# Turning the MLP operand row tile by row tile behind the out-projection, and computing two of three token bands of the first up product there

## The reference

```python
o = jnp.concatenate([group_rms(oa), group_rms(ob), group_rms(oc)], axis=-1) * g_out
x = layer_norm(ALPHA * x + g1 * (o @ w_out)) * ln1_g + ln1_b
u = layer_norm(x) * (1 + sc2) + sh2
f = jnp.square(jax.nn.relu(u @ w1)) @ w2
x = layer_norm(ALPHA * x + g2 * f) * ln2_g + ln2_b
```

## Time and profile before

| | us |
|---|---|
| Median of three runs | 3206.3 (3202.11 to 3210.19) |
| The profiled execution | 3209.08 |
| Its span, first to last instruction | 3207.3 |
| TensorE busy | 2925.9 (91%) |
| VectorE busy | 1589.9 (50%) |
| ScalarE busy | 874.6 (27%) |
| GpSimd busy | 1514.6 (47%) |
| Mean granted TensorE clock | 0.935 of full |

### The profile page before, as it was taken

The page is one execution under the profiler, slowest core; times in us unless marked ns, Lnnn a source line. Parts: engine busy times, 40 slices in busy tenths (PEclk is TensorE's granted clock), DMA queues, the critical chain, the costliest instruction groups (busy, mean ns, idle before and its releaser), DMA issues. The chain is left out here.

```text
span 3207.3 us, 46999 instructions
## 1 busy us (share of the span) xinstructions
PE 2925.9 (91%) x18646; PEld 2794.3 (87%) x18646; DVE 1589.9 (50%) x3213; ACT 874.6 (27%) x1710; POOL 1514.6 (47%) x680
## 2 busy tenths in 40 slices
PE   5999899787899999999979998987979999999993
PEld 5999789565899999999979897985759999999993
DVE  6552677457433333333675418765654333333347
ACT  1331476325200110011253317653341010011001
POOL 2693596125334343434339818942434343434334
PEclk6999899889899999999769999997989999999996
DMA  5451211422111111110534402113211111111112
GB/s 227 163 171 54 76 45 44 141 85 77 59 47 44 47 39 52 39 52 26 201 146 148 170 16 88 50 49 143 101 61 53 40 50 41 50 42 41 51 43 92
DMA packets 117351, 253.63 MB, mean 79 GB/s; under 512 B 42564, under 2 KB 78952, under 8 KB 103700
## 3 DMA queue, kind: packets, MB, share of 16 engines
q1 hardware_dynamic: 110868, 228.58, 20.8%
q10 hardware_dynamic: 6336, 23.07, 2.0%
HBM read 217.19 MB, written 42.19 MB: 81 GB/s over the span
## 5 line engine op out<-in xcount | busy, mean ns | idle before, releaser
L378 PE MATMUL psum<-u_hi,w_hi 128*128 128x352 f32 x2016 | 650.7, 323 | 3.6 <-DVE v_rows L1245 3.6
L378 PE MATMUL psum<-u_lo,w_hi 128*128 128x352 f32 x2016 | 651.8, 323 | 0.0
L378 PE MATMUL psum<-u_hi,w_lo 128*128 128x352 f32 x2016 | 650.9, 323 | 0.0
L2168 DVE SCALAR_TENSOR_TENSOR acc_t<-psum,mods,acc_t 128x704 f32<-128x704 f32 x720 | 376.0, 577 | 275.2 <-PE psum L378 275.2
L378 PE MATMUL psum<-h_hi,w_lo 128*128 128x352 f32 x1536 | 495.3, 322 | 0.0
L378 PE MATMUL psum<-h_lo,w_hi 128*128 128x352 f32 x1536 | 495.0, 322 | 0.0
L378 PE MATMUL psum<-h_hi,w_hi 128*128 128x352 f32 x1536 | 494.3, 322 | 0.0
L357 POOL CAST w_hi<-w_raw 128x2048 fp32r<-128x2048 f32 x72 | 136.3, 1893 | 656.5 <-DVEq L2161 357.4
L2151 DVE TENSOR_TENSOR h_relu<-h_relu 128x1056 f32<-128x1056 f32 x64 | 112.2, 1753 | 634.3 <-ACT h_relu L2141 634.3
L378 PEld LDWEIGHTS psum<-u_hi,w_hi 128*128 128x128 f32 x2016 | 379.4, 188 | 4.9 <-issue 4.6
L378 PEld LDWEIGHTS psum<-u_lo,w_hi 128*128 128x128 f32 x2016 | 379.6, 188 | 0.0
(11 more groups left out here) (269 smaller groups left out, 5571.4 us busy)
## 6 DMA issues: line engine op xcount, KB each, us to landing
w_raw<-in_w_all SPq DMA_DIRECT2D x86, 1024.0 KB, 4.8
w_ada_b<-in_w_ada_t ACTq DMA_DIRECT2D x44, 512.0 KB, 3.5
w_ada_v<-in_w_ada_t SPq DMA_DIRECT2D x20, 512.0 KB, 3.3
row_tiles<-in_x_prompt SPq DMA_DIRECT2D x16, 512.0 KB, 12.7
scr_o<-o_head SPq DMA_DIRECT2D x32, 256.0 KB, 2.6
row_tiles<-scr_o SPq DMA_DIRECT2D x16, 512.0 KB, 16.0
x_between_norms<-row_tiles SPq DMA_DIRECT2D x16, 512.0 KB, 2.6
mlp_rows<-x_between_norms SPq DMA_DIRECT2D x16, 512.0 KB, 7.2
```

The costliest lines, as they stand in the source:

```text
L378: mm = pe.matmul(out[:, b, :], w[s][:, c:c + P], a[:, k, b * NB:(b + 1) * NB], start=(k == 0 and w is w_hi and a is a_hi), stop=(k == n - ...
L2168: ins = dve.scalar_tensor_tensor(a, y, mods[:, 40 + m, c:c + 1], a, ALU.mult, ALU.add)
```

## The change

- The MLP block no longer turns the operand. In the out-projection block TensorE turns one row tile at a time, all 8 depths, into `wide[3]` (`turn_tile`): tile 0 ahead of out-projection tile 3, then tile t - 2 behind out-projection tile t, tiles 7 and 8 later. It waits for the tile's second norm and for the last turned tile to be read.
- ScalarE reads depths 0 to 3 of the turned tile in four operations with scale and shift, VectorE depths 4 to 7 in two, and VectorE makes the high part of all 8 (`read_half`). GpSimd makes the low part (`low`). The unsplit columns (`u_raw`) take the place of the out-projection's `u_lo`, and `u_lo` is written over them.
- The loops of ScalarE and VectorE have a new order (`out_act`, `out_dve`): second sums of tile j - 1, roots and first norm of tile j, second norm of tile j - 1, read of tile j - 2. The helpers in them compute what they did in `chain_act` and `chain_dve`.
- GpSimd splits chunk UP0 ahead of its first gain, into a buffer of its own (high) and in place over raw buffer 0 (low).
- Bands 0 and 1 (352 tokens each) of the first up product are done at the end of the out-projection block (`first_up`), band 2 at the start of the MLP block. There SyncE waits for it before it loads chunk UP0 + 2 over the low part, and GpSimd splits chunk UP0 + 1 as soon as it has landed.

```diff
+        u_raw = at("u_rows_turned", U0 + 33792, [P, KT, T])
+        up_hi = at("w_up_hi", Q0, [P, CW], F32R)
+        up_lo = at("w_up_lo", W0, [P, CW], F32R)
...
+            FED = 2 * (KT + 1)
+            def first_up(pe, b):
+                for m in range(2):
+                    for k in range(KT):
+                        c = 256 * k + P * m
+                        for w, a in ((up_hi, u_hi), (up_lo, u_hi), (up_hi, u_lo)):
+                            mm = pe.matmul(lin[m][:, b, :], w[:, c:c + P], a[:, k, b * NB:(b + 1) * NB],
+                                           start=(k == 0 and w is up_hi and a is u_hi), stop=(k == KT - 1 and a is u_lo))
+                    if b == 2:
+                        mm.then_inc(h_mm, 1)
...
+            def out_act(act, u, junk_rows):
...
+                def read_half(t):
+                    act.wait_ge(t_turned, FED + t + 1)
+                    for k in range(KT // 2):
+                        ins = act.activation(u_raw[:, k, t * P:(t + 1) * P], psum[:, 6, k * P:(k + 1) * P], ACT.Identity,
+                                             bias=mods[:, 24 + k, 0:1], scale=mods[:, 32 + k, 0:1])
+                    ins.then_inc(t_read, 1)
+                for j in range(NTT):
+                    if j >= 1:
+                        second_sums(j - 1)
+                    roots(j)
+                    if j < NPT:
+                        first_norm(j)
+                    if j >= 1:
+                        second_norm_of(j - 1)
+                    if j >= 2:
+                        read_half(j - 2)
+                roots(NTT)
+                read_half(NPT - 1)
+            def out_dve(own, u):
...
+                def read_half(t):
+                    h, c = KT // 2, slice(t * P, (t + 1) * P)
+                    dve.wait_ge(t_turned, FED + t + 1)
+                    own.did(dve.tensor_tensor(u_raw[:, h:KT, c], psum[:, 7, :].rearrange("p (k c) -> p k c", c=P),
+                                              gains(32 + h, h, 0, P), ALU.mult), u_half)
+                    own.settle()
+                    own.did(dve.tensor_tensor(u_raw[:, h:KT, c], u_raw[:, h:KT, c], gains(24 + h, h, 0, P), ALU.add))
+                    own.settle()
+                    dve.wait_ge(t_read, FED + t + 1)
+                    own.did(dve.tensor_copy(u_hi[:, :, c], u_raw[:, :, c]), u_high)
+                for j in range(NTT):
+                    sum_rows(j)
+                    if j == NTT - 1:
+                        dve.sem_inc(w_used, OUT_CH)
+                    dve.wait_ge(f_root, (NTT + 1) * u + j + 1)
+                    refine(j, None, f_fig)
+                    if j == NTT - 1:
+                        break
+                    if j >= 1:
+                        second(j - 1)
+                    if j >= 2:
+                        read_half(j - 2)
+                t, x = NPT, x_all[0:DEC, NPT, :]
+                second(NPT - 1)
+                normed(x, t, None)
...
+                own.did(dve.tensor_tensor(x, x, ln_g[0:DEC, :], ALU.mult))
+                own.settle()
+                own.did(dve.tensor_tensor(x, x, ln_b[0:DEC, :], ALU.add), f_last)
+                own.settle()
+                read_half(NPT - 2)
+                own.settle()
+                first_figures(t)
...
+                normed(x, t, f_xs)
+                read_half(NPT - 1)
...
@@ the out-projection block, gpsimd @@
+                    pool.wait_ge(t_lo, 2 * (KT + 1))
+                    pool.wait_ge(raw_in[0], UP0 * 8 + 16)
+                    pool.tensor_copy(up_hi[:], raw[0][:, 0:CW]).then_inc(pool_step, 1)
+                    pool.wait_ge(pool_step, 2 * UP0 + 1)
+                    pool.tensor_tensor(up_lo[:], raw[0][:, 0:CW], up_hi[:].bitcast(F32), ALU.subtract).then_inc(pool_step, 1)
...
+                    def low(t):
+                        x = (slice(None), slice(None), slice(t * P, (t + 1) * P))
+                        pool.wait_ge(u_high, t + 1)
+                        pool.tensor_tensor(u_lo[x], u_raw[x], u_hi[x].bitcast(F32), ALU.subtract).then_inc(t_lo, 1)
                     pool.wait_ge(f_ln, 32 * (USE + 1))
-                    chain_pool(own, USE, 0, NPT)
-                    pool.wait_ge(f_last, USE + 1)
-                    pool_weights(pool, UP0, 1)
+                    for t in range(NPT):
+                        chain_pool(own, USE, t, t + 1)
+                        if t >= 2:
+                            low(t - 2)
+                    low(NPT - 2)
+                    low(NPT - 1)
@@ tensor @@
+                    def turn_tile(t):
+                        if t >= 1:
+                            pe.wait_ge(t_read, FED + t)
+                            pe.wait_ge(u_half, t)
+                        if t < NPT:
+                            pe.wait_ge(f_xn, NTT * USE + t + 1)
+                        else:
+                            pe.wait_ge(f_xs, 1)
+                        r = rows_of(t)
+                        for k in range(KT):
+                            mm = pe.transpose(wide[3][:, k * r:(k + 1) * r], x_all[0:r, t, k * P:(k + 1) * P], ident[0:r, 0:r])
+                        mm.then_inc(t_turned, 1)
+                    turn_tile(0)
                     for t in range(3, NTT):
                         pe.wait_ge(f_ev, NTT * USE + t - 2)
...
                         mm.then_inc(f_mm, 1)
+                        turn_tile(t - 2)
+                    pe.wait_ge(w_ready, UP0 + 1)
+                    pe.wait_ge(f_ev, NTT * USE + NTT - 1)
+                    pe.wait_ge(t_lo, FED + 3)
+                    first_up(pe, 0)
+                    turn_tile(NPT - 1)
+                    pe.wait_ge(f_ev, NTT * USE + NTT)
+                    pe.wait_ge(t_lo, FED + 6)
+                    first_up(pe, 1)
+                    turn_tile(NPT)
@@ the MLP block, sync @@
                     sp_weights(sp, l, UP0 + 1, 1)
+                    sp.wait_ge(h_mm, 2)
                     sp_weights(sp, l, UP0 + 2, 2 * MLP_BLK - 2)
@@ gpsimd @@
-                    pool.wait_ge(t_lo, 2 * (KT + 1) + 6)
                     pool_weights(pool, UP0 + 1, 1)
@@ tensor @@
-                            turned_project(pe, 2, n, s, h_mm)
+                            first_up(pe, 2)
@@ scalar, vector @@
-                    read_turned_rows(act, 2, 32, 24)
-                    split_turned_rows(Own(dve, dve_step), 2, 32, 24)
-                    dve.wait_ge(t_lo, 3 * (KT + 1))
```

More of the change, by code:

```diff
@@ L546, in build @@
         f_fig2, f_last = S("f_second_figures"), S("f_sample_x1")
+        u_half, u_high, f_xs = S("u_half_read_vector"), S("u_tiles_high"), S("f_sample_normed")
         f_st = [S(f"rows_stored{i}") for i in range(4)]
@@ new lines, in out_act, with roots, norm, second_sums @@
+            def out_act(act, u, junk_rows):
+                own = Own(act, act_step)
+                def roots(n):
+                    t = min(n, NPT)
+                    r = rows_of(t)
+                    act.wait_ge(f_var, (NTT + 1) * u + n + 1)
+                    own.did(act.activation(fig[0:r, 1, t:t + 1], fig[0:r, 0, t:t + 1], ACT.Ln))
+                    own.settle()
+                    own.did(act.activation(fig[0:r, 2, t:t + 1], fig[0:r, 1, t:t + 1], ACT.Exp, scale=-0.5), f_root)
+                def norm(t, done):
+                    x = x_all[:, t, :]
+                    own.did(act.activation(x, x, ACT.Identity, bias=fig[:, 3, t:t + 1], scale=fig[:, 4, t:t + 1]), done)
+                def second_sums(t):
+                    x = x_all[:, t, :]
+                    act.wait_ge(f_x1, NPT * u + t + 1)
+                    own.settle()
+                    own.did(act.activation(junk_rows[:], x, ACT.Copy, accum_out=fig[:, 5, t:t + 1]))
+                    own.settle()
+                    own.did(act.activation(fig[:, 6, t:t + 1], fig[:, 5, t:t + 1], ACT.Copy, scale=-1.0 / D))
+                    own.settle()
+                    own.did(act.activation(junk_rows[:], x, ACT.Square, bias=fig[:, 6, t:t + 1], accum_out=fig[:, 0, t:t + 1]))
+                    own.settle()
+                    own.did(act.activation(fig[:, 1, t:t + 1], fig[:, 0, t:t + 1], ACT.Ln, scale=1.0 / D, bias=eps[:]))
+                    own.settle()
+                    own.did(act.activation(fig[:, 2, t:t + 1], fig[:, 1, t:t + 1], ACT.Exp, scale=-0.5), f_sum)
+                def first_norm(t):
+                    act.wait_ge(f_fig, NTT * u + t + 1)
+                    norm(t, f_yn)
+                def second_norm_of(t):
+                    act.wait_ge(f_fig2, NPT * u + t + 1)
+                    act.wait_ge(f_st[t % 4], stored(t, u))
+                    norm(t, f_xn)
+                def read_half(t):
[16 more added lines that the diff above has]
+                read_half(NPT - 1)
@@ L2027, in _ @@
                     act.activation(gate_s[:], wide[3][0:DEC, :], ACT.Copy).then_inc(f_gate, 1)
-                    chain_act(act, USE, row_junk, False)
+                    out_act(act, USE, row_junk)
```

(3 more changed lines are left out.)

67 lines of the change are left out of this document (added).

## The result

| | before | after |
|---|---|---|
| Median, us | 3205.72 (4 runs, 3202.11 to 3210.19) | 3245.85 (4 runs, 3237.18 to 3246.59) |
| Ratio | | 1.0116, interval 1.01 to 1.0133 |
| The profiled execution | 3209.08 | 3246.59 |
| Its span | 3207.3 | 3244.8 |
| Mean granted TensorE clock | 0.935 | 0.929 |

The change makes the kernel slower by 40 us in the medians and 37.5 in the two profiled executions. The forecast was 3239 (3241.6 for a run like the profiled one). Three of the four runs after lie at 3245.64 to 3246.59; the fourth, 3237.18, has no profile, so what it lacked is open, and a difference of a few us between medians of four runs says little by itself. In the kernel after, most lines are moved: L1972 is L2179, L378 is L381, the gain and bias are L680 and L682, the norms L1950.

What follows compares the result with a forecast made beforehand. The prediction took TensorE, busy 91% of the span, as the bound, time being lost where it stands or runs at low clock. Losses of 17.0 and 15.5 us in the two layers, 32.5 on 3206.3, gave 3239, range 3222 to 3256.

Steps and rivals of the forecast that it cites:

- Step 1: First turning: GpSimd's split makes the row chain 14.1 us late, holding TensorE 30.1 us ahead of out-projection tile 3.
- Step 2: After the long hold TensorE's clock is low: 3.8 us at half pace, costing 1.9 us.
- Step 3: Out-projection up to tile 8: a 12.8 us cycle, VectorE's copy held by GpSimd; tile 8 ends at 823.2, 38.3 later.
- Rival B: VectorE's high part not held by GpSimd's gain and bias: cycle 12.0, tail 6.6 us a layer shorter, 3226; chance 0.15.
- C: Rival: GpSimd is slowed by VectorE as well, cycle 13.8, 7 us a layer more, 3253; chance 0.16.
- Step 4: Out-projection block's end: TensorE stands 5.5 us before turning 7 for VectorE's half read; next block begins at 851.6.
- Step 5: Next block: 3.9 us wait for second-chunk weights plus 1.7 clock; second up product 17.0 us later, 15.5 in layer 1.
- Rival D: First up chunk is there when GpSimd asks: chain on time, 14.1 us a layer come back, 3211; chance 0.06.
- Rival E: No hold ahead of tile 3, only the tail counts: 15 to 16.5 us won each layer, 3175; chance 0.05.
- A: The forecast itself: late first chunk, cycle 12.8, late second chunk; 3239, between 3230 and 3248; chance 0.58.

Runs made afterwards that it cites:

- e1: The changed kernel with TensorE's turning of tile 0 moved from ahead of out-projection tile 3 to behind it; 3239.86 us, ratio 1.0101.
- e3: The changed kernel with the moves of e1 and e2 together; 3221.73 us, ratio 1.0045.
- e2: The changed kernel with GpSimd's split of the first up chunk moved behind tile 2's gain and bias and the first low part; 3219.24 us, ratio 1.0036.
- e4: e3 with VectorE's shift and high part behind the next tile's sums, GpSimd's low parts one tile later, split ahead of the first; 3208.98 us, ratio 1.0013.
- e8: The changed kernel with VectorE's half read, shift and high part of tile 6 ahead of the sample tile's work; 3241.67 us, ratio 1.0109.
- b0: The kernel before, unchanged, profiled once more; 3205.99 us, ratio 0.9998.
- e5: The changed kernel's same operations with the orders of all four engines rewritten; 3182.32 us, ratio 0.9928 to the kernel before.
- e6: e5 with the second up chunk loaded in the out-projection block, right behind the first; 3177.43 us, ratio 0.9918 to the kernel before.

## Why the prediction was right, and where its terms were off

**Step 1 (the first turning) holds in what happens, with too high a price.** The first chunk landed 14.4 us after its issue (715.52 to 729.90; 15.1 taken), the gain began at 736.69 with the 1.8 us of shift in it (forecast 735.8), TensorE was held 28.5 instead of 30.1. But what costs is the lateness of the chain, and the hold is only its shadow: e1 cuts the hold in two and leaves the second up product where it was, and e3, with both moves, gives no more than e2. The lateness was not paid in full. In e2 the first gain starts 13.3 us earlier, counted from the last attention turning, and the second up product 9.7 and 9.9: the split still takes its 6.6 us of GpSimd, now ahead of tile 3's gain, and turning 2 waits 2.7 for it.

**Step 2 (clock)** is as forecast: the four microseconds from 748 ran at 0.50.

**Step 3 (pace) is right for the row chain and wrong for TensorE.** The chain's cycle is 12.57 a tile, not 12.8, and VectorE's hold, which the step puts in it, is shown by e4: 0.69 against 2.78 for the same copy. ScalarE's four reads took 1.48, not the 1.2 of my row. TensorE itself takes 12.0 from turning to turning (762.50 to 774.50), so the row chain's longer cycle reached it only at turning 6, 0.4 late, and not by 0.8 a tile. Tile 8 was done at some 822.7, 820.9 without the shift, where 823.2 was forecast (the step's own terms, five tiles of 12.8 behind 761.9, would even give 825.9). In this kernel the long hold had given the chain a lead; in e3, without it, TensorE waits some 0.3 us ahead of each of the turnings 3 to 6. Rival B, no hold, falls, though up to turning 5 TensorE went at B's 12.0, and C, a cycle of 13.8, is right only in kind: GpSimd's bias is slowed from 2.40 to 2.73, 0.3 us a tile. Of this hold the Trainium skill (SBUF — State Buffer, "SBUF: two separate sides") says that the pair of SBUF ports that VectorE and GpSimd share is locked exclusively and that the one that starts first keeps it for its whole instruction. The trace agrees: the held shift and copy end 0.55 us behind the GpSimd instruction that they wait for, GpSimd's bias is longer where it begins under VectorE's shift, and the 128x8 operation takes 0.16 or 1.95 by whether it starts ahead of a GpSimd instruction or inside one.

**Step 4 (tail)** has its size right and its lever wrong. Turning 7 waited 4.9 (forecast 5.5) and the next block began at 850.4, 848.6 without the shift (forecast 851.6, 3 us too late, 2.3 of it from step 3). I named VectorE's half read behind the sample's chain as what it hangs on; e8 moved that, and ScalarE's half read, behind tile 7's second norm, stood there 3.4 us. So moving VectorE's work alone can't bring back the 7 us of the step; e8 brought 0.2.

**Step 5 (weights)** was 3.1 for 3.9, with matmuls 0.29 apart behind it. The second up product began at 863.03 and, with the clock, worked as if at 865.8, that is 17.6 behind before, where 17.0 was forecast; less the 1.8 it is 15.8. Layer 1 was 11.8 for 15.5: its second product came at full clock, without the 2.7 of layer 0. The 1.5 us that the step takes off there was chance of the one profile (b0 has 814.1 for 815.6); against b0 layer 1 lost 13.3.

**Rival D** needed the chunk at once and fell by the landing time. **Rival E** (no hold, 3175, faster than before) fell for the kernel as it is. But its layout, the tail alone, is what e5 and e6 come near with 3182 and 3177, after the order of all four engines was changed for it. I had taken 16 us as the least hold; e2 has 15.3, and it is that much only while turning 0 stands ahead of tile 3.

**What was missing** is the attention of layer 1. The blocks give 27.6 us where the sum had 32.5; the 8.3 in unchanged code and 1.8 of scatter ahead of the first block bring it to the 37.5 of the two profiled executions, within 0.2. That the total came within 7 us is in part luck: terms that were too large and a term that wasn't there lean against each other. The blocks alone would give 3234, still nearer to A than to B.

## What to carry to other kernels

When work is put ahead of a chain on one engine, charge the chain's delay to the end of the block (here 9.8 of 13.3 us came back when it was taken away) and don't count the stand of the engine that waits for it again; moving the waiting instruction only splits the stand. Ask of a wait on two releasers how late the second is before the first is moved. Before work is taken for too much, try it in another order: here 39 us of waits became 14 with the same instructions, and operations of VectorE that GpSimd holds (2.78 us for 0.69) belong in its gaps.

## What the runs showed of the hardware

A VectorE operation can be held by GpSimd however small it is: a 128x8 sum of 0.16 us took 1.95, a 32x1024 norm of 0.80 took 2.88. Not all are held: a multiply from PSUM beside GpSimd's low part kept its 1.22, and in the kernel before the pair of sums of a tile (L387, 1.29 us from 722.68) and the variance (L755, 0.15 us at 724.24) lie inside GpSimd's gain and its bias and take what they take elsewhere. GpSimd pays as well, 2.73 for 2.40 where its bias begins under VectorE's shift. And a shift of a quarter of a microsecond between two engines goes with such a hold, and in the kernel after with 17 us at half clock behind it, in code that nobody touched; it is in the profiles of nine changed kernels of nine, and its cause is open. The attention is 4.5 to 8.3 us longer there, of the size of many a tuning step.
